# An encoder layer on eight cores: the first tile's convolution spread over three engines, the pool map folded into the output projection, pair sums, and constant rows spread by matmuls

## The reference, cut to what matters

```python
z = x @ w_in + b_in                       # 1024 -> 512 (u) + 512 (a) + 512 (g)
v = a * sigmoid(g)                        # GLU
d = trailing_mean(u, windows 2/4/8/16) - u          # one window per group of 128 channels
pool = einsum('blgc,gcd->blgd', d, w_pool).reshape(...) * pool_scale
conv = silu(layer_norm(depthwise_conv(v, 31 taps) + conv_b))     # 512 channels
h = layer_norm(alpha * x + concat(pool, conv) @ w_out + b_out)
y = layer_norm(alpha * h + relu(h @ w_up)**2 @ w_down)           # 1024 -> 4096 -> 1024
```

## Time and profile before

| quantity | value |
|---|---|
| median of three runs (lowest, highest) | 2548.84 us (2547.84, 2615.7) |
| the profiled execution's own time | 2545.76 us |
| its span, slowest core (others 2533.2 to 2544.0) | 2544.7 us |
| granted clock of TensorE, mean, slowest core | 0.982 |
| busy share: PE, DVE, ACT, POOL | 95%, 74%, 47%, 51% |
| DMA: moved, mean rate | 483 MB, 190 GB/s |

### The profile page before, as it was taken

One profiled execution on the slowest core, in us unless ns is written; L12 is line 12 of the kernel. 1 busy time (PEld: TensorE's weight loads), 2 busy tenths in 40 slices (PEclk: granted clock), 3 DMA queues, 4 the chain that ended last, 5 costly groups with the idle time before them and its releaser, 6 DMA issues.

```text
span 2544.7 us, 39217 instructions; the slowest of 8 cores (2533.2 to 2544.7 us)
## 1 busy us (share of the span) xinstructions
PE 2419.2 (95%) x11688; PEld 1142.7 (45%) x11908; DVE 1894.2 (74%) x3170; ACT 1203.7 (47%) x1918; POOL 1302.3 (51%) x1065
## 2 busy tenths in 40 slices
PE   4298999999999999999999999999999999999998
PEld 2043444444444444444444444444444444454645
DVE  5895595968869596886959678695877959693851
ACT  4363372735437263543726355372635527262533
POOL 4761392744629264462926436282653728264543
PEclk9599999999999999999999999999999999999999
DMA  9599978764755656464565645556564555565676
GB/s 172 133 137 207 234 199 216 224 199 161 189 211 176 198 180 202 159 186 179 182 199 182 199 158 185 188 182 195 181 203 146 185 188 181 189 200 178 228 250 234
DMA packets 79184, 483.17 MB, mean 190 GB/s; under 512 B 11808, under 2 KB 12064, under 8 KB 29760
## 3 DMA queue, kind: packets, MB, share of 16 engines
q1 hardware_dynamic: 70912, 422.41, 47.2%
q0 software_dynamic: 7344, 55.61, 14.4%
q10 hardware_dynamic: 720, 2.62, 0.4%
HBM read 486.68 MB, written 55.82 MB: 213 GB/s over the span
## 4 chain that ended last, share of the span: by engine, by line
PE 90%; DMA 4%; DVE 3%; issue 2%; ACT 0%; another core or an unknown queue 0%; POOL 0%; DVEq 0%; ACTq 0%; POOLq 0%; SPq 0%
PE bank L486 88%; DMA sb_wring<-wblk 2%; DVE bank L714 1%; DMA sb_wring<-wscr 1%; PE bank L940 1%; DMA sb_rb<-wblk 1%; PE bank L809 1%; PE bank L806 0%; DVE sb_acc L839 0%; DVE sb_stat L1004 0%; DVE sb_xr L1002 0%; DVE sb_xr L1044 0%; DVE sb_xr L1047 0%; ACT sb_rb L899 0%
## 5 line engine op out<-in xcount | busy, mean ns | idle before, releaser
L763 DVE SCALAR_TENSOR_TENSOR bank<-sb_vext,sb_params,bank 128x512 f32<-128x512 f32 (+1 forms) x1856 | 1169.5, 714 | 0.1
L486 PE MATMUL bank<-sb_wring,sb_rb 128*128 128x512 bf16 x4092 | 904.8, 380 | 6.8 <-DMA sb_wring<-wscr 3.1
L486 PE MATMUL bank<-sb_hT,sb_wring 128*128 128x512 bf16 (+2 forms) x4231 | 883.7, 368 | 22.2 <-DMA sb_wring<-wblk 15.4
L486 PEld LDWEIGHTS bank<-sb_hT,sb_wring 128*128 128x128 bf16 x4320 | 423.4, 98 | 479.7 <-issue 27.1
L486 PEld LDWEIGHTS bank<-sb_wring,sb_rb 128*128 128x128 bf16 (+1 forms) x4160 | 405.8, 98 | 497.2 <-issue 11.6
L977 ACT ACTIVATE sb_rtmp<-bank 128x512 f32<-128x512 f32 (+2 forms) x544 | 308.7, 571 | 185.0 <-PE bank L486 180.9
L978 ACT ACTIVATE sb_rb<-sb_rtmp 128x512 bf16<-128x512 f32 (+2 forms) x544 | 323.4, 604 | 41.2 <-ACT sb_rtmp L977 2.6
L922 POOL TENSOR_TENSOR sb_stat<-sb_stat,sb_cst 128x1 f32<-128x1 f32 x128 | 71.2, 556 | 519.1 <-DVE sb_stat L920 518.8
L486 PE MATMUL bank<-sb_xT,sb_wring 128*128 128x512 bf16 (+2 forms) x1477 | 314.0, 366 | 1.4
L1002 DVE TENSOR_TENSOR sb_xr<-bank,sb_xr 128x512 f32<-128x512 f32 x130 | 89.5, 688 | 284.7 <-PE bank L486 284.7
L864 POOL TENSOR_TENSOR sb_xr<-sb_xr,sb_row 128x1024 f32<-128x1024 f32 (+1 forms) x65 | 152.4, 2370 | 246.2 <-DMA sb_xr<-xp 246.1
(11 more groups left out here) (87 smaller groups left out, 1772.8 us busy)
## 6 DMA issues: line engine op xcount, KB each, us to landing
sb_wring<-wscr SPq DMA_DIRECT2D x323, 1024.0 KB, 5.2
sb_xr<-xp SPq DMA_DIRECT2D x64, 512.0 KB, 7.8
yp<-sb_xr SPq DMA_DIRECT2D x64, 512.0 KB, 2.8
sb_wring<-wblk POOLq DMA_DIRECT2D x27, 1024.0 KB, 13.2
sb_xT<-xpt POOLq DMA_DIRECT2D x14, 1024.0 KB, 10.6
wscr<-sb_wring SPq DMA_DIRECT2D x12, 1024.0 KB, 8.9
wscr<-wblk POOLq DMA_DIRECT2D x6, 1024.0 KB, 27.1
wscr<-sb_rb SPq DMA_DIRECT2D x3, 1024.0 KB, 14.7
```

The source lines that it names most:

```text
L486: ins = q.eng.matmul(o, l(), r(), start=first and i == 0, stop=last and i == len(items) - 1)
L763: yield Op(dve, tap(Tp), lambda e: e.scalar_tensor_tensor(out=o.ap[:, 0:Tp], in0=src.ap[:, k:k + Tp], scalar=wk, in1=p.ap[:, 0:Tp], op0=AL ...
```

## The change

- **Tile 0's convolution.** Chunk 3 goes to PE: 31 float32 matmuls of 128x512, each with a diagonal 128x128 matrix of one tap's weights, which ACT makes from a float32 identity (six buffers, `sb_diag`); ACT adds the bias when it copies the sum out. Chunk 1 is ACT products and POOL adds for taps 0 to 19 (KP = 20, so 19 adds); its last 11 taps are DVE's, with both inputs and the output in SBUF (`sb_vext`, `sb_acc`). Chunks 0 and 2 stay DVE's.
- **Pair sums.** Two chunks' sums and two chunks' squares (now float32, `sb_sqf`) are added before `stats`, which has four matmuls instead of eight; ACT's four copies a tile go. The adds are DVE's in tiles 0 to 3 and POOL's from tile 4 on.
- **Pool map.** `w_pool` times `pool_scale` is multiplied into the top half of `w_out` once, in tile 0: four 512 KB float32 loads by SP, four scalings by ACT, eight float32 matmuls (`fold`), eight casts by ACT into the ring slots of blocks 3 and 4, whose bottom halves alone are now cast by POOL's queue. The trailing means go straight to `sb_mix` chunks 0 to 3; the four matmuls and four ACT instructions a tile go.
- **Constant rows.** Five 4 KB loads to one partition, ten float32 matmuls with a row of ones (`spread`), ten ACT copies.
- **Weights.** `LATE` changes; blocks 3 and 4 are stored to the scratch in tile 0. The first four `DIRECT` casts are issued behind block 7's cast, each waiting as `paced` says; before, they stood behind tile 0's `stats`, all four in a row.

```diff
-LATE = {1: 1, 3: 2, 4: 1, 2: 2, 6: 1, 9: 2, 12: 3, 15: 1, 18: 3}
+KP = 20
+LATE = {1: 1, 6: 1, 15: 1, 2: 2, 9: 2, 18: 2, 7: 3, 12: 3}
 DIRECT = (13, 14, 16, 17, 19, 20)
...
+        def spread():
+            for i in (4, 0, 1, 2, 3):
+                banks_ = [Val(R, 1), Val(R, 1)]
+                for h in range(2):
+                    o = banks_[h]
+                    items = [(lambda: ones_f[0:1, :], lambda: rows[i][0:1, h * 512:(h + 1) * 512], [cv["onesf"], cv[f"raw{i}"]])]
+                    yield group(lambda: o.ap[:], o, items, 0.9)
...
+                if kind == "direct":
+                    r = paced(wsv[b])
+                    yield Op(pool, 0.6, lambda e: e.dma_start(out=wscr[b], in_=wblk[b]), r, [wsv[b]], prio=0, sem=dsem(), mb=2.1)
...
+                elif key in ((0, 3), (0, 4)):
+                    w = wo_v[b - 3][0]
+                    r = paced(w)
+                    yield Op(pool, 0.6, lambda e: e.dma_start(out=w.ap[:, 2048:4096], in_=wblk[b][:, 2048:4096]), r, [w],
+                             prio=0, sem="load2", mb=1.05)
...
+        def fold_loads():
+            for g in range(4):
+                yield Op(sp, 0.06, lambda e: e.dma_start(out=wo_f[g].ap[:].rearrange("p (b n) -> p b n", b=2),
+                                                         in_=wblk[3:5, :, g * 512:(g + 1) * 512].rearrange("b p n -> p b n")),
+                         [fmark], [wo_f[g]], prio=1, sem="load", mb=0.53)
+        def fold_scale():
+            for g in range(4):
+                yield Op(act, 0.3, lambda e: e.activation(out=wpf[:, g * 128:(g + 1) * 128], in_=wpf[:, g * 128:(g + 1) * 128],
+                                                          func=AF.Identity, bias=0.0, scale=pcol(P_PSC, g)), [wps[g], cv["params"]], [wps[g + 1]], 3)
+        def fold():
+            for h in range(2):
+                for g in range(4):
+                    o = Val(R, 1)
+                    items = [(lambda: wpf[:, g * 128:(g + 1) * 128], lambda: wo_f[g].ap[:, h * 512:(h + 1) * 512], [wps[4], wo_f[g]])]
+                    yield group(lambda: o.ap[:], o, items, 0.9)
+                    S.spawn(fold_out(h, g, o))
+        def fold_out(h, g, o):
+            a, b = wo_v[h][g], wo_v[h][g + 1]
+            yield Op(act, ac(512), lambda e: e.copy(out=b.ap[:, g * 512:(g + 1) * 512], in_=o.ap[:]), [o, a], [b], 3)
         def scratch_rb(flat, vals, b):
             yield Op(sp, 0.06, lambda e: e.dma_start(out=wscr[b], in_=flat), vals, [wsv[b]], prio=1, sem=dsem(), mb=1.05)
-        def scratch_store(v, b):
...
+            def conv0_dve(self, c, k0=0, p=None):
...
+                for k in range(k0, KC):
...
+                    home = ACC[c] if k0 else C
...
+                for k in range(KP):
...
+                S.spawn(self.conv0_dve(c, KP, p))
...
+                    yield Op(act, 0.33, lambda e: e.activation(out=dg[k].ap[:], in_=identf[:], func=AF.Identity, bias=0.0, scale=wk),
+                             [cv["ident"], cv["params"]], [dg[k]], 6)
...
+            def conv0_pe(self, c):
+                T, src = self.T, self.v[c]
+                dg = [Val(DG, 1) for _ in range(KC)]
+                S.spawn(self.conv0_diag(c, dg))
+                p = None
+                for k in range(KC):
+                    o = Val(R, 1, over=p)
+                    items = [(lambda: dg[k].ap[:], lambda: src.ap[:, k:k + T], [self.v[c], self.vh[c], dg[k]])]
+                    yield group(lambda: o.ap[:, 0:T], o, items, 0.9, over=p, first=k == 0, last=k == KC - 1)
+                    p = o
+                S.spawn(self.conv0_end(c, p))
...
+            def pairsum(self, p):
                 T = self.T
-                a, cb, qb = self.acc[c], self.cb[c], self.qb[c]
-                yield Op(act, ac(T), lambda e: e.copy(out=cb.ap[:, 0:T], in_=a.ap[:, 0:T]), [a], [cb], 2)
-                yield Op(act, ac(T), lambda e: e.activation(out=qb.ap[:, 0:T], in_=a.ap[:, 0:T], func=AF.Square), [a], [qb], 2)
+                a, b, cb = self.acc[2 * p], self.acc[2 * p + 1], self.cb[p]
+                q, d = (dve, dv(T)) if self.m < 4 else (pool, 0.23 + 0.00203 * T)
...
+                for i in range(2):
...
+                    a = self.acc[2 * p + i]
+                    yield Op(act, ac(T), lambda e: e.activation(out=s[i].ap[:, 0:T], in_=a.ap[:, 0:T], func=AF.Square), [a], [s[i]], 2)
+                qb = self.qb[p]
...
+                    for c in range(2):
                         q.deps([self.cb[c].phys, cv["ones"].phys], [self.s1.phys] if c == 0 else [])
-                        q.eng.matmul(self.s1.ap[:, 0:T], ones_bf[:], self.cb[c].ap[:, 0:T], start=c == 0, stop=c == 3)
...
+                    for c in range(2):
                         q.deps([self.qb[c].phys], [self.s2.phys] if c == 0 else [])
-                        ins = q.eng.matmul(self.s2.ap[:, 0:T], ones_bf[:], self.qb[c].ap[:, 0:T], start=c == 0, stop=c == 3)
...
-            def poolmap(self):
-                T = self.T
-                for g in range(4):
-                    o = Val(R, 1)
-                    items = [(lambda: wpool_bf[:, g * 128:(g + 1) * 128], lambda: self.d[g].ap[:, 0:T], [self.d[g], cv["wpool"]])]
-                    yield group(lambda: o.ap[:, 0:T], o, items, mm(1, T))
...
-            for b in range(3):
-                yield from t0.inproj(b, ("f", b))
+            yield from t0.inproj(0, ("f", 0))
+            yield from t0.inproj(1, ("f", 1))
+            yield from spread()
+            for c in range(t0.nch):
+                S.spawn(t0.xload(c))
+            yield from t0.inproj(2, ("f", 2))
+            yield from t0.conv0_pe(3)
             for i in range(n_ptiles + 1):
                 t = tiles[i - 1] if i else None
...
-                                    yield from nx.poolmap()
...
+                if i == 0:
+                    yield from t0.stats()
                 yield from n2.inproj(0, k2(0))
                 if i == 0:
-                    for c in range(t0.nch):
-                        S.spawn(t0.xload(c))
-                    yield from t0.stats()
-                    S.spawn(direct(DIRECT[0:4]))
-                    yield from t0.poolmap()
+                    yield from fold()
                 for h in range(2):
                     yield from nx.wout(h, (i, 3 + h))
```

More of the change, by code:

```diff
@@ new lines, in spread, with spread_out @@
+        def spread():
[5 more added lines that the diff above has]
+                    yield group(lambda: o.ap[:], o, items, 0.9)
+                S.spawn(spread_out(i, banks_))
+        def spread_out(i, banks_):
+            f = {0: ALPHA, 1: ALPHA, 4: 1.0 / ALPHA}.get(i, 1.0)
+            for h in range(2):
+                o = banks_[h]
+                yield Op(act, ac(512), lambda e: e.activation(out=rows[i][:, h * 512:(h + 1) * 512], in_=o.ap[:], func=AF.Copy, scale=f),
+                         [o], [cv[f"row{i}" if h else f"half{i}"]], 3)
@@ L731, in conv0_pool @@
                     if k:
[L732 removed]
+                        w = Val(ACC[c], 1)
                         w.over = p if k > 1 else None
@@ L1085, in build @@
                 order.append(((i, b), b, 4 if b < 13 else t.nch, kind(i, b)))
+                if i == 0 and b == 7:
+                    for d in DIRECT[0:4]:
+                        order.append((None, d, 0, "direct"))
         za, zb = [k for k, x in enumerate(order) if x[0] in ((n_ptiles - 1, 3), (n_ptiles - 1, 4))]
@@ L1183, in build @@
         late_consts()
+        fmark = Val(P(None, "fmark"), INF)
+        wo_f = [Val(XR, 2) for _ in range(4)]
+        wps = [cv["wpf"]] + [Val(cv["wpf"].phys, 1) for _ in range(4)]
+        for a, b in zip(wps, wps[1:]):
+            a.left, b.over = 1, a
+        wps[4].left = 8
+        wo_v = []
+        for key in ((0, 3), (0, 4)):
+            chain = [Val(RING, 1) for _ in range(4)] + [ring_vals[key]]
+            for a, b in zip(chain, chain[1:]):
+                b.over = a
+            wo_v.append(chain)
+        S.spawn(row_loads())
+        S.spawn(fold_loads())
+        S.spawn(fold_scale())
         S.spawn(ring_thread(order))
```

120 lines of the change are left out of this document (67 added, 53 removed).

## The result

The changed kernel takes 2508.0 and 2508.8 us; against 2547.1 to 2548.8 us before, the ratio is 0.9851 with an interval of 0.9835 to 0.9867. That is some 38 us, where 53 were forecast. Two more executions, 2694.8 and 2749.7 us, with one die at a lower granted clock throughout, make the plain median of the four 2601.8; such executions are left out, and of e5 to e8, e10 and e12, where most executions were like that, only the order of events in tile 0 and the cores that kept their clock are read.

A forecast was written before the change was run, and what follows sets the result against it. PE bounds the kernel, apart from waits in tile 0 and for weights. Terms 24.2 + 0.9 + 10 (tile 0) + 18 make 53 us, giving 2496 us; own range 2489 to 2504, wide range 2482 to 2522.

The forecast's parts named there:

- Steady tiles: Tiles 1 to 14 and the 272-frame tile: eight matmuls fewer per tile, 1.73 us each full tile, 24.2 + 0.9 us.
- Weights after tile 0: From tile 0's up projection to the next input block: earlier direct casts regain 18 of 19.9 us lost.
- PE's float32 chain: Tile 0 on PE: new float32 matmuls let the sums end no sooner than 49.3 + 41x, 73.9 us, under 96.
- x: Time in us of one float32 matmul on PE; taken as 0.6, bounds 0.216 and 1.73.
- that rival: Float32 matmuls bind in tile 0: at x 1.73 the up projection starts at 173.3, total time 2529 us; chance 0.15.
- the slower one: Same float32 chain in tile 0, dearer: break-even at x = 2.14, at 2.6 the total time is 2571 us; chance 0.03.
- The step that failed: Tile 0, DVE: each of eleven pairs of chunk 1 and chunk 2 taps takes 1.6 us beside POOL, 17.6 in all.
- 20 us of cover: Tile 0, POOL: casts may delay trailing means, wanted at 109.5; only delay beyond 20 us costs, one to one.
- the 19th add: Tile 0, POOL's last add for chunk 1, ahead of DVE's eleven taps: ends at 67, between 63 and 70.
- the tail behind the pairs: Tile 0: pair sums, two more taps, squares and four short matmuls after the last pair, 5.8 to 11.2 us.
- late weights: After tile 0: direct casts wait for landings ahead of ring loads, the 18 us stay lost, 2514 us; chance 0.15.
- The end: Last tile: its end is left as it is, so it gains nothing.

The follow-up runs named there:

- e5: Changed kernel with chunk 1's last eleven taps accumulating in PSUM and fold loads issued ahead of the input rows' loads; median 2548.29 us beside 2595.2 for the kernel before.
- e8: Changed kernel with chunk 1 all ACT products and POOL adds, chunk 3 still on PE; group median 2553.49 us beside 2595.2.
- e10: e5 with chunk 1's 20 products first in ACT's queue (priority 1 instead of 7); ratio 0.9874, interval 0.9808 to 0.994.
- e12: The kernel of e5 measured once more; median 2571.38 us beside 2624.01 for the kernel before.
- e9: Changed kernel with the four direct casts issued in a row when tile 0's output projection starts, not behind block 7; 2521.26 us.
- e2: Changed kernel with POOL's four row adds of tile 0 waiting for chunk 1's last tap, order on each engine unchanged; 2505.85 us.
- e4: Changed kernel with POOL's four row adds of tile 0 made as eight of 512 columns; 2508.33 us.

## Why the prediction was right where it was, and where not

- **Steady tiles**: right, in mechanism and size. 147.69 us a tile; POOL's pair adds hid, with PE waiting 0.6 and 0.3 us for them in the last tile alone. (The prediction's reason, that PE waited for the sums once, leaves out three more waits of 0.3 to 1.7 us in the kernel before; they lie in tile 0 and the last tile, so the reason holds for the steady ones.)
- **Weights after tile 0**: right in mechanism and near in size. The stretch gained 17.8, of which 1.7 are tile 1's matmuls, so 16.1 stand against 18. e9 shows that the place of the direct casts did it.
- **PE's float32 chain**: x was taken as 0.6 and is 22.48 / 26 = 0.865, four times the 0.2159 of a bf16 matmul. The diagonals ended at 87.5, so it did not decide, as forecast; that rival and the slower one were off by the size of x. The estimate from the Trainium skill ("FP8 and Floating Point Precision", section "TensorE Precision Notes"), 0.86, agrees. The ten rows took 1.25 each, with a granted clock of 0.71 from 39 to 51 us, behind PE's waits of 18.0 and 2.6 us.
- **The step that failed** is "I take the pair as long as one such product, 1.6 us: 17.6 us". The mechanism was named and the size was off: 30.5 us, which alone is 12.9 of the 13.4 us by which the up projection came late. The price was a mean of unlike things: the 1.71 behind it mixes two normalizations of 0.70 with two of 2.83, so the longest that the rows held, a stand of one row add, was not seen. With trailing means alone beside the taps, e9 does find the forecast's size, 17.65. With direct casts among the means two taps take 4 us (e2 keeps those), and with row adds behind each other one takes 7 (e2, e4). The Trainium skill ("SBUF — State Buffer", section "Who interferes with whom") names an exclusive lock, and says of DVE's two-port modes that the engine that issues first holds it for its whole instruction. The traces agree that one stands while the other works (7.07 against 0.75 with POOL silent); that the one that stands can stand for three instructions, or six, the measurement adds.
- **Two terms were not independent.** The place of the direct casts that gave the time back behind tile 0 cost 10.6 us in it: e9 takes it away, with some of the means in another order, and gets 142.75 where the forecast had 140. I had costed them on POOL as a delay with 20 us of cover, not by what they do to the tap on the other side.
- **The smaller parts**: the 19th add came 4.6 us late (71.6), as ACT's copies of the rows waited for PE ahead of the products (e10); the tail behind the pairs was 5.9 instead of 11.2; from the sums to the output projection it was 15.9 instead of 13.5, now PE's own block and fold (9.26 + 7.03). They nearly cancel.
- **Luck**: 2508 lies outside the forecast's own range, 2489 to 2504. It lies in the wide one, 2482 to 2522, since that was drawn to take in late weights (2514), and the weights were not late. The time was covered, but for another reason than the one it was widened for.
- **The end**: 0.6 lost instead of nothing. The last tile's sums wait for DVE and POOL, and PE's 24 matmuls behind that took 7.05 instead of 5.44 us; this was read only, not tried.
